# A two-block transformer in split fp32 on one core: RMS factors multiplied in behind the projections, residual tiles split as they are added

## What is computed

```
h = x * rsqrt(mean(x*x) + eps) * g          # rmsnorm, g per feature
block a: h @ w_in -> 8-head attention over the 128 keys that an indexer picks, and attention over mem;  x += out @ w_out
ffn 0:   a, b = split(h @ w_up);  x += (silu(conv3(a)) * b) @ w_down
block b: windowed attention with 16 heads of 64, and attention over mem;  x += out @ w_out
ffn 1:   as ffn 0;  then x = rmsnorm(x, g_final)
conv:    b, c, u, z = split(h @ w_in);  x += (b * conv3(c*u) * silu(z)) @ w_out
last:    compressed, selected and window keys from rmsnorm(x, kv_norm), queries and gates from
         rmsnorm(x, b_norm); three-branch attention;  x += out @ w_out;  out = rmsnorm(x, final_norm)
```

## Time and profile before

| | before |
|---|---|
| median of 3 runs | 2473.98 us (2472.59 to 2474.97) |
| profiled execution, span from first to last instruction | 2479.7 us |
| TensorE matmul busy | 2301.5 us, 93% |
| VectorE, ScalarE, GpSimd busy | 47%, 42%, 11% |
| matmuls | 10890 |
| mean granted TensorE clock | 0.95 of full |
| HBM traffic | 181.9 MB, 73 GB/s |
| chain that ended last | TensorE 83%, VectorE 6%, issue 4%, ScalarE 3% |

### The profile page before, as it was taken

One profiled execution on the slowest core, in us unless ns is written; L12 is line 12 of the kernel. 1 busy time (PEld: TensorE's weight loads), 2 busy tenths in 40 slices (PEclk: granted clock), 3 DMA queues, 4 the chain that ended last, 5 costly groups with the idle time before them and its releaser, 6 DMA issues.

```text
span 2479.7 us, 34233 instructions
## 1 busy us (share of the span) xinstructions
PE 2301.5 (93%) x10890; PEld 1867.0 (75%) x10890; DVE 1169.4 (47%) x2407; ACT 1038.5 (42%) x1943; POOL 271.6 (11%) x174
## 2 busy tenths in 40 slices
PE   5986999899999899989999989999998789999998
PEld 4775777788888677778888868888887667777776
DVE  5685442555532566345553244444433562444443
ACT  4333452455532366345553222222222435465651
POOL 3032221100000211110000110000001100011111
PEclk8998999899999999989999989999999889898988
DMA  3122112232333210223333323223222322000001
GB/s 118 52 79 65 60 51 68 71 99 93 102 98 104 64 40 26 77 68 101 93 97 98 102 68 99 96 93 101 93 94 84 102 76 85 10 19 9 18 9 68
DMA packets 50051, 182.92 MB, mean 74 GB/s; under 512 B 5552, under 2 KB 5680, under 8 KB 49840
## 3 DMA queue, kind: packets, MB, share of 16 engines
q1 hardware_dynamic: 49824, 181.35, 22.7%
q0 software_dynamic: 144, 0.52, 0.1%
HBM read 179.76 MB, written 2.10 MB: 73 GB/s over the span
## 4 chain that ended last, share of the span: by engine, by line
PE 83%; DVE 6%; issue 4%; ACT 3%; POOL 2%; DMA 1%; DVEq 0%; ACTq 0%; POOLq 0%; SPq 0%
PE pj L1677 67%; PE ps L1806 5%; PE po L1862 4%; PE pt L1822 2%; ACT w_hi L666 1%; PE ps L1978 1%; PE po L1847 1%; DVE w_lo L1086 1%; PE pj L1773 1%; DVE s_sb L1239 1%; DMA raw<-in_wstream 1%; DVE rtmp L1190 1%; PE po L1871 1%; POOL r L546 1%; DVE hf L1169 0%
## 5 line engine op out<-in xcount | busy, mean ns | idle before, releaser
L1677 PE MATMUL pj<-h_hi,w_hi 128*128 128x512 f32 x1736 | 710.0, 409 | 19.0 <-DVE h_lo L1155 16.2
L1086 DVE TENSOR_TENSOR w_lo<-raw,w_hi 128x1024 fp32r<-128x1024 f32 x288 | 352.8, 1226 | 788.1 <-ACT w_hi L666 780.8
L1677 PE MATMUL pj<-h_lo,w_hi 128*128 128x512 f32 x1736 | 687.5, 396 | 0.0
L1677 PE MATMUL pj<-h_hi,w_lo 128*128 128x512 f32 x1736 | 687.2, 396 | 0.0
L666 ACT ACTIVATE w_hi<-raw 128x1024 fp32r<-128x1024 f32 x334 | 353.5, 1059 | 637.4 <-PE pj L1677 619.9
L1677 PEld LDWEIGHTS pj<-h_hi,w_hi 128*128 128x128 f32 x1736 | 332.8, 192 | 94.5 <-issue 20.3
L1677 PEld LDWEIGHTS pj<-h_hi,w_lo 128*128 128x128 f32 x1736 | 332.8, 192 | 71.7
L1677 PEld LDWEIGHTS pj<-h_lo,w_hi 128*128 128x128 f32 x1736 | 333.8, 192 | 65.3 <-issue 1.7
L1677 PE MATMUL pj<-G_hi,w_hi 128*128 128x512 f32 x704 | 281.5, 400 | 4.1 <-DVE G_lo L1298 3.0
L1677 PE MATMUL pj<-G_lo,w_hi 128*128 128x512 f32 x704 | 280.2, 398 | 0.0
L1677 PE MATMUL pj<-G_hi,w_lo 128*128 128x512 f32 x704 | 279.9, 398 | 0.0
(11 more groups left out here) (259 smaller groups left out, 2546.3 us busy)
## 6 DMA issues: line engine op xcount, KB each, us to landing
raw<-in_wstream SPq DMA_DIRECT2D x334, 512.0 KB, 3.5
xT<-in_x SPq DMA_DIRECT2D x4, 512.0 KB, 7.1
out_x<-xT SPq DMA_DIRECT2D x4, 512.0 KB, 2.7
memT<-in_mem SPq DMA_DIRECT2D x1, 1024.0 KB, 10.5
cst<-in_cst SPq DMA_DIRECT2D x1, 515.5 KB, 3.6
tab<-in_tab POOLq DMA_DIRECT2D x1, 512.0 KB, 4.9
posi<-in_pos SPq DMA_DIRECT2D x1, 256.0 KB, 2.8
vec<-in_vec SPq DMA_DIRECT2D x1, 179.0 KB, 8.5
```

The lines of the kernel that those rows point to most:

```text
L1086: nc.vector.tensor_tensor(w_lo[:, here], raw[:, here], w_hi[:, here].bitcast(f32), ALU.subtract).then_inc(lo_ready, 1)
L1677: mm = nc.tensor.matmul(acc, w[:, col:col + P], x[part], start=first and k == 0, stop=last and k == 2)
```

## The change

The factor of a norm is the same for all features of a token, so it can be multiplied in behind a projection. x times gain is split as it stands: ScalarE writes h_hi right after a residual tile is added (`gained`), VectorE h_lo (`lowest`), before it makes the last w_lo of that tile. TensorE projects these tiles and makes the column sums behind 7 of the 8 blocks of the first chunk and the spread behind 5 of the second (`first_two`). GpSimd now adds all eight squares. ScalarE copies the spread factor to SBUF (`spread_factor`). It is multiplied in by VectorE: as a product of its own in the up loops (two per trip), the conv loop (three per trip, with the scaling of x by final1, which moves into every second trip), for values, keys and queries of the last block, gates and nz; through rope tables that hold the factor already in blocks a and b (`tables_by_factor`); through the scale of exp for the attention over mem; and for ckv in its own root (rck). The queries of nq are taken by VectorE instead of ScalarE. At the start gains, x and the first two weight chunks are loaded first, and x is split while its squares are made; mem's sums and spread come behind later chunks. The core of the diff:

```diff
-            sp.dma_start(posi[:, :], posin).then_inc(ld["pos"], 16)
-            sp.dma_start(cst[:, :], cstin).then_inc(ld["cst"], 16)
+            sp.dma_start(vec[:, :], vecin).then_inc(ld["vec"], 16)
...
                 sp.dma_start(xT[:, here], xin[:, here]).then_inc(x_loaded[m // 2], 16)
-            sp.dma_start(vec[:, :], vecin).then_inc(ld["vec"], 16)
+                if m in (0, 4):
+                    par = m // 4
+                    sp.dma_start(raw[:, par * CW:(par + 1) * CW],
+                                 wstream[par:par + 1, :, :].rearrange("a p c -> p (a c)")).then_inc(chunk_loaded[par], 16)
+            sp.dma_start(posi[:, :], posin).then_inc(ld["pos"], 16)
+            sp.dma_start(cst[:, :], cstin).then_inc(ld["cst"], 16)
             sp.dma_start(memT[:, :], memin).then_inc(ld["mem"], 16)
-            with sp.Fori(0, NCHUNKS // 2) as i:
+            with sp.Fori(1, NCHUNKS // 2) as i:
...
-                for m in range(1, DT - 1):
+                for m in range(1, DT):
...
+            def gained(name, i, j):
+
+                _, _, gain, first, hi, _ = NORM[name]
+                m = i * 2 + j
+                scale = gg[:, sl(m, 1)] if name == "conv" else vec[:, sl(m + VC[gain] + first, 1)]
+                settle(act)
+                nc.scalar.activation(hi[:, sl(m * S, S)], xT[:, sl(m * S, S)], ACT.Copy,
+                                     scale=scale).then_inc(hhi_ready, 1)
...
                 act.wait_ge(x_ready, RESIDUALS[BEHIND[name]] + m + 1)
+                if name != "final2":
+                    gained("conv" if name == "final1" else name, i, j)
                 if not isinstance(m, int) or m >= 2:
-                    act.wait_ge(rest_summed, (DT - 2) * list(BEHIND).index(name) + m - 1)
+                    act.wait_ge(rest_summed, (DT - 1) * list(BEHIND).index(name) + m - 1)
                 settle(act)
                 nc.scalar.activation(sq[:, j * S:(j + 1) * S], xT[:, sl(m * S, S)], ACT.Square).then_inc(sq_ready, 1)
...
+                    act.wait_ge(conv_ready, i + (l * FT + 1))
...
+            act.wait_ge(ld["vec"], 16)
+            for m in range(DT):
+                act.wait_ge(x_loaded[m // 2], 16)
+                gained("amix", m // 2, m % 2)
+                if m >= 2:
+                    act.wait_ge(rest_summed, m - 1)
+                nc.scalar.activation(sq[:, (m % 2) * S:(m % 2 + 1) * S], xT[:, m * S:(m + 1) * S],
+                                     ACT.Square).then_inc(sq_ready, 1)
+                if m in (1, 5):
+                    split_hi(At(m // 4))
             tables(0)
-            split_hi(At(0))
...
             c, t = At(CH["afront"]), At(TL["afront"])
             split_hi(c + 2)
+            act.wait_ge(rest_used, 1)
             take(qn[:, 0:S], t, c)
+            spread_factor("amix")
+            split_hi(c + 3)
...
+            def lowest(name, m, j):
+
...
+                here = sl(m * S, S)
+                settle(dve)
+                nc.vector.scalar_tensor_tensor(out=lo[:, here], in0=xT[:, here], scalar=scale,
+                                               in1=hi[:, here].bitcast(f32), op0=ALU.mult,
+                                               op1=ALU.subtract).then_inc(h_ready[j], 1)
...
+            def scaled(name, dst, t, n=S):
+
+                nc.vector.tensor_tensor(dst, pj[t.par][:, 0:n], fac[name][:, 0:n], ALU.mult).then_inc(pj_free[t.par], 1)
...
+            def take_query(ph, i, j):
+
+                c, t = query_at(ph, i, j)
+                dve.wait_ge(chunk_used, c.v + 3)
+                scaled("kv2", qn[:, j % 2 * S:(j % 2 + 1) * S], t)
...
+                if name == "nq":
+                    dve.wait_ge(silu_ready, CT + dict(STAGES)["nz"])
+                    for j in range(2):
+                        take_query(ph, 0, j)
...
 
+                name = {"down0": "bmix", "down1": "conv", "cout": "kv2"}.get(stage)
+
                 def two(i, last=False):
                     for j in range(2):
-                        for k in range(per):
+                        for k in range(per - 1):
                             split_lo(At(CH[stage] + j * per + k + 2, i, 2 * per))
                         c, t = At(CH[stage] + (j + 1) * per - 1, i, 2 * per), At(TL[stage] + j, i, 2)
...
                         dve.sem_inc(x_ready, 1)
+                        if name:
+                            lowest(name, i * 2 + j, j)
...
                         split_lo(At(CH[stage] + c + 2))
                     t = At(TL[stage] + j)
...
+                    lowest({"aout": "affn", "bout": "bffn"}[stage], j, j % 2)
+                    split_lo(At(CH[stage] + chunks_of(j)[-1] + 2))
...
+                means(("affn", "bffn")[l])
+                have_factor(("affn", "bffn")[l])
                 with dve.Fori(0, FT) as i:
-                    link.begin(i, 2)
+                    link.begin(i, 3)
                     c, t = At(up, i, 2), At(base, i, 2)
                     split_lo(c + 2)
 
                     complete(c)
                     w = [VD("f_conv_w", i + (l * 3 + j) * FT) for j in range(3)]
-                    a = pj[t.par]
-                    link(nc.vector.tensor_scalar(fa[:, :], a[:, :], w[2], VD("f_conv_b", i + l * FT), ALU.mult, ALU.add))
-                    link(nc.vector.scalar_tensor_tensor(out=fa[:, 1:S], in0=a[:, 0:S - 1], scalar=w[1], in1=fa[:, 1:S],
+                    scaled(("affn", "bffn")[l], fr[:, :], t)
+
...
                                                         op0=ALU.mult, op1=ALU.add))
-                    nc.vector.scalar_tensor_tensor(out=fa[:, 2:S], in0=a[:, 0:S - 2], scalar=w[0], in1=fa[:, 2:S],
-                                                   op0=ALU.mult, op1=ALU.add).then_inc(pj_free[t.par], 1)
+                    nc.vector.scalar_tensor_tensor(out=fa[:, 2:S], in0=fr[:, 0:S - 2], scalar=w[0], in1=fa[:, 2:S],
+                                                   op0=ALU.mult, op1=ALU.add).then_inc(conv_ready, 1)
                     split_lo(c + 3)
...
 
+                    dve.wait_ge(act_ready, i + (l * FT + 1))
+                    link(nc.vector.tensor_tensor(fb[:, :], fb[:, :], fac_f[:, :], ALU.mult))
                     complete(c + 1)
-                    dve.wait_ge(act_ready, i + (l * FT + 1))
 
                     dve.wait_ge(g_ready, i + (l * FT + 1))
...
+                lowest("amix", m, m % 2)
+                if m in (1, 5):
+                    split_lo(At(m // 4))
             dve.wait_ge(ld["pos"], 16)
             link(nc.vector.tensor_copy(posf[:, :], posi[:, :]))
             dve.wait_ge(ld["cst"], 16)
             angles(0)
             means("amix")
-            dve.wait_ge(ld["vec"], 16)
-            nc.vector.tensor_scalar(nsink[:, :], vec[:, VC["sinks"]:VC["sinks"] + 16], -1.0, None, ALU.mult)
-            split_lo(At(0))
-            apply("amix")
-            split_lo(At(1))
+            split_lo(At(2))
+            dve.wait_ge(rs_ready, 1)
+            link(nc.vector.tensor_copy(rsa[:, 0:NB], r4[:, 0:NB]))
+            nc.vector.tensor_tensor(rsq[:, 0:NB], rsa[:, 0:NB], rsa[:, 0:NB], ALU.mult)
...
 
 
-            norm("bmix")
+            means("bmix")
+            dve.wait_ge(rs_ready, STATS.index("bmix") + 1)
+            nc.vector.tensor_scalar(rsm[:, 0:NB], r4[:, 0:NB], ATT["bmem"].scale, None, ALU.mult)
+            have_factor("bmix")
...
                 if k < 2:
-                    link(rope(ktmp[:, 0:S], qraw[:, :], tab64, SHUF64, t))
+                    link(rope(ktmp[:, 0:S], qraw[:, :], tab_b, SHUF64, t))
                     spread_keys(b_k, k).then_inc(roped, 1)
+                else:
+                    complete(c)
+                    if k == 3:
+                        dve.wait_ge(v_turned, TN["bv"] + 1)
+                    scaled("bmix", vraw[:, :], t)
             attention("bq")
             attention("bmem")
...
+            have_factor("conv")
+            link(nc.vector.tensor_tensor(fac2[:, :], fac_f[:, :], po[0][:, :], ALU.mult))
+            with dve.Fori(0, CT // 2) as i:
...
+                    dve.wait_ge(pj_free[(t + 1).par], (t + 1).half + 2)
+                    link(nc.vector.tensor_tensor(fb[:, :], fb[:, :], fac2[:, :], ALU.mult))
...
+                    complete(c + 2)
+                    nc.vector.tensor_tensor(zr[:, :], pj[t.par][:, :], fac_f[:, :], ALU.mult).then_inc(pj_free[t.par], 1)
+                    split_lo(c + 4)
+                    if e == 0:
+                        here = xT[:, ds(i * S, S)]
...
+            def take_kv(k):
+
+                c, t = At(CH["cmp_kv"] + k), At(TL["cmp_kv"] + k)
+                complete(c)
+                if k >= 2:
+                    dve.wait_ge(folded, k - 1)
+                here = slice(t.par * S, t.par * S + S)
...
+                take_kv(k)
+            dve.wait_ge(folded, 2)
+            window(0)
+            window(1)
+            for k in range(2):
+                split_lo(At(CH["cmp_kv"] + k + 4))
+                take_kv(k + 2)
```

(38 more changed lines are left out.)

367 lines of the change are left out of this document (211 added, 156 removed).

## The result

The changed kernel takes **2488.19 us** (median of 4, 2487.14 to 2490.17) against 2474.47 us (median of 4, 2472.59 to 2475.34) for the kernel before: ratio 1.0057, interval 1.0043 to 1.0071. It is slower by 0.57%, or 13.7 us. I had said 2475 us, no change, with 2436 to 2496 as the range. The profiled execution has a span of 2486.6 us.

A forecast was written before the change was run, and what follows sets the result against it. TensorE, busy for 93% of the span, was taken as the bound, with gains left at stage boundaries. The terms, 22 - 17 - 2 - 8 + 3 + 4 - 4 + 2, summed to 0: 2475 us, range 2436 to 2496.

The forecast's parts named there:

- the chain of the up loop: Up-loop trip over ScalarE and VectorE: two added products lengthen it from 10.48 to 11.85 us, above TensorE's 10.88.
- the end of up0: From aout's end to the first up loop's end: 264.5 us instead of 253.4, +11; with bout and up1, +22.
- the third cmp chunk: From cout's end to this chunk: 44.0 us instead of 51.6, -8 (-12 to -3).
- the first indexer score: At the start: this score at 68 us instead of 72.0, -4 (-10 to +2), with TensorE starting at about 9.
- the slack behind the residual tiles: Five stages of 8 tiles: w_lo split ready at 5.05 us, needed after 5.4 to 5.6; it still fits, 0.
- Rival B: Up loops stay TensorE-bound because a table load leaves the chain: 39 us less, 2436 us; chance 0.13.
- Rival C: Splits behind the residual tiles come 0.6 us late at 39 tiles: +23 us, 2498 us; chance 0.17.
- bq and bmem: Stages behind the last turn of v in bfront: no change, 0.
- nz and nq: Attention nq: VectorE takes two queries before the first rope, +3.5, and six more takes, +0.5: +4 (+1 to +7).
- nkv and q2: Behind the third cmp chunk: VectorE takes over ScalarE's work, about +2 and +1.5, q2 tiles -0.5: +3 (0 to +5).
- The down stages, cout and nout: Lengths of down0, down1, cout and nout: no change, 0.
- conv: From down1's end: third conv chunk after about 15.1 us instead of 31.8, -17 (-18 to -13); loop's added products cost nothing.

The follow-up runs named there:

- first trace: The profiled execution of the unchanged kernel before, from which the prediction's sum was made; span 2479.7 us.
- the second: The kernel before traced once more, with no edit; span 2474.8 us.
- silu_first: The changed kernel with one Silu of a single column ahead of each up loop; 2447.87 us, ratio 0.988 against the kernel before.

## Why the prediction was right or wrong

**Right, term by term:** the chain of the up loop (11.85 us said, 11.80 measured; the bounds of 11.7 and 12.25 are not what the prediction's own terms give, which is 11.6 and 12.1) and with it the end of up0 (264.5 and 263.7 us after aout); the third cmp chunk (44.0 and 44.1 us after cout); the end of bfront (37.8 and 37.5); the first indexer score (68 and 68.5, though TensorE's first projection came at 12.1 and not at 9); the conv loop that hides its products; the slack behind the residual tiles. Rival B (0.13) did not come about: the load stayed in the loop. But its mechanism was true, since taking the load out gives 40 us, where it said 39. (The 40 have 1.5 us of the tiles' place in them.) Rival C (0.17) did not come about either, with 0.2 to 0.4 us to spare.

ScalarE: Activation LUTs (What ACT_TABLE_LOAD costs) of the Trainium skill would make the up loops 58 us longer over both stages by its drain. They got 20 us longer, and the load cost 1.31 us in the chain. Here the measurement decides: the load's own duration and nothing more.

**Wrong: the last step, from the sum to the median.** I took the sum (0) against the trace of 2479.7 us and then predicted 2475, next to the median, as if the two kernels' traces stood equally to their medians. They did not. Wherever a traced execution was timed too, its time is 1.8 to 1.9 us above its span, so the first trace's would be about 2481.6 us (an estimate): 7.1 us above the median of 2474.47. The changed kernel's traced execution took 2488.41 us, 0.2 above its median. The first trace had one more low stretch of the clock in nq, 7.2 us, than the second, which was timed at 2476.71. Half of the 13.7 us is this. The prediction named the 0.2% between trace and median and took it as the same for both kernels.

**Mis-sized terms, the other 7 us.**

- bq and bmem: 0 said, +3.5. TensorE stood 6.30 and 3.06 us for v, runs the first 3 us of the query projections behind the second wait at the low clock (granted 0.90 over these 12.3 us, where it was 1.00), and has another low stretch of 3 us behind them; I had stopped counting the low clock at the last turn. Some 1 us of it is the first trace's own, since the second one has 156.8 us there.
- nz and nq: +4 said, +7.0. The wait was 4.90 us for 3.5, the first 19.8 us of nq run at the low clock throughout (granted 0.50, where it was 0.64), and nz begins low (+1.3) behind the gates' wait.
- nkv and q2: +3 said, +4.8. The scaled v was queued behind ScalarE's split as well.
- The down stages, cout and nout: 0 said, +1.7 in four stages whose matmuls wait for nothing. Their pitch, the time between two matmul starts, depends on where the tiles lie, and the change's new small tiles move G_hi and G_lo by 128 bytes.
- conv: -17 said, -15.2. The third chunk came at 16.6 us, not 15.1. The two spreads were through at 13.8 us and not at 12.7: TensorE had waited 0.80 us for GpSimd's second sum and then ran eight matmuls at the low clock (0.43 us apart), which the term had left out. The chunk then waited 0.40 us for its w_lo:

```profile
1477.83 0.69 DVE L1651 TENSOR_TENSOR fac<-fac_f,po 128x512 f32<-128x512 f32 x1 [2.15 <-ACT fac_f L708]
1478.73 1.22 DVE L1117 TENSOR_TENSOR w_lo<-raw,w_hi 128x1024 fp32r<-128x1024 f32 x1 [0.22 <-ACT w_hi L678]
1480.01 0.50 PE L1835 MATMUL pj<-h_hi,w_hi 128*128 128x512 f32 x1 [0.40 <-DVE w_lo L1117]
```

That split waited for ScalarE's. The product of the two factors, which was not in my sum, had ended 0.2 us before and cost nothing here.

Against all these stand up loops 2 us shorter than said and a shorter aout and bout (-1.9, not explained).

**How much the hit is worth.** The measured time lies inside the range, but the range is 60 us wide because it takes in B and C. The forecast value was 13 us too low, with the direction left open (0.39 for slower was its largest share).

**The rest of the price.** silu_first alone turns the change from 0.57% slower to 1.2% faster than the kernel before: the boundaries, conv and cmp were won nearly as forecast, and one instruction ahead of a loop decided the sign.

## What to carry to other kernels

Before putting work into a loop that TensorE fills, write down the chain of the other engines beside it with its slack, and look for a link that costs nothing today (a table load at the loop's head, a product behind a wait): it gets its full price on the day the slack is gone, and one instruction ahead of the loop may take it out. Scale a tile that another engine waits for ahead of a split, not behind it, and count what the split itself waits for. When the sum is made on one trace, take a second trace of the same kernel first: a difference between them is part of the error of every prediction.

## What the runs showed of the hardware that I had not expected

- Matmuls with operands in G_hi and G_lo follow each other after 0.2333 us or after 0.2289 us, by nothing but the place of the tiles (32 bytes), and after 0.2343 us in the changed kernel (128 bytes): 2% of a stage that TensorE fills, 5 us over the two down stages.
- In nq the granted clock drops to 0.50 for 7 to 24 us at a time, in one execution once more than in another, with the same instructions: 7.2 us between the two traces.
- A wait of TensorE can cost more or less than itself. 12.7 us of waits taken away gave some 16 us; 4.9 us taken away gave only 3 to 3.6. Which it is depends on what the clock does behind it, and from these traces I could not say beforehand.
